# Modulation chunks folded in three places, and the bias diagonals shared between two engines, in a fused decoder trunk

## The reference, cut to what matters

```python
for l in range(DEPTH):
    mod = jax.nn.silu(c) @ ada_w[l] + ada_b[l]
    sh1, sc1, g1, sh2, sc2, g2 = jnp.split(mod[:, None, :], 6, axis=-1)
    h = rmsnorm(x, norm1_g[l]) * (1.0 + sc1) + sh1
    x = x + g1 * hybrid_mixer(h, positions, rel_bias, ...)
    h = rmsnorm(x, norm2_g[l]) * (1.0 + sc2) + sh2
    x = x + g2 * peer_ffn(h, ...)
```

## Time and profile before

| | |
|---|---|
| median of 3 runs | 2330.95 us (2330.95 to 2333.8) |
| profiled execution | 2331.92 us, span 2330.1 us |
| mean granted clock, share of full | 0.956 |
| busy | PE 2155.0 us, DVE 1545.6, ACT 1229.2, POOL 439.4 |
| DMA | 378.78 MB, mean 163 GB/s |

### The profile page before, as it was taken

How to read it: one execution, slowest core, us unless ns; L and a number is a source line. 1 busy time by engine, 2 the same in 40 slices (tenths; PEclk the granted TensorE clock), 3 DMA queues, 4 the chain that set the end, 5 groups by cost and what they waited for, 6 DMA issues and landing times.

```text
span 2330.1 us, 39430 instructions
## 1 busy us (share of the span) xinstructions
PE 2155.0 (92%) x13500; PEld 1948.3 (84%) x13500; DVE 1545.6 (66%) x3026; ACT 1229.2 (53%) x2330; POOL 439.4 (19%) x184
## 2 busy tenths in 40 slices
PE   5788779999999999999998877999999999999998
PEld 4677668999999988888877766899999998888886
DVE  7669436993577867777766943699347886555555
ACT  8622424555688854444442242445468885454553
POOL 0000016889300000000000001678930000000000
PEclk9789789999999999999999977999999999999999
DMA  7733034455444447777763303445544444556553
GB/s 257 264 100 100 28 129 136 154 181 172 144 136 144 142 142 259 263 266 256 266 223 106 100 28 109 132 154 182 170 140 145 139 137 131 195 191 194 193 191 107
DMA packets 103474, 378.78 MB, mean 163 GB/s; under 512 B 11488, under 2 KB 11872, under 8 KB 102880
## 3 DMA queue, kind: packets, MB, share of 16 engines
q1 hardware_dynamic: 102672, 373.74, 48.0%
q10 hardware_dynamic: 720, 4.00, 0.4%
HBM read 375.46 MB, written 2.23 MB: 162 GB/s over the span
## 4 chain that ended last, share of the span: by engine, by line
PE 65%; issue 14%; POOL 9%; DVE 7%; ACT 2%; DMA 2%; POOLq 0%; SPq 0%; DVEq 0%; ACTq 0%
PE bank L1626 30%; POOL split_lo L478 9%; PE bank L1529 7%; PE bank L1530 7%; PE bank L1531 7%; PE bank L1593 5%; PE bank L1318 3%; DMA ring<-stream 2%; PE bank L1281 1%; PE bank L1492 1%; PE bank L1292 1%; PE bank L1343 1%; DVE grid L841 1%; DVE grid L974 1%; PE bank L1616 1%
## 5 line engine op out<-in xcount | busy, mean ns | idle before, releaser
L1529 PE MATMUL bank<-h_hi,split_hi 128*128 128x256 f32 x2304 | 670.1, 291 | 40.6 <-DVE h_lo L1080 21.3
L1530 PE MATMUL bank<-h_lo,split_hi 128*128 128x256 f32 x2304 | 655.8, 285 | 0.0
L1531 PE MATMUL bank<-h_hi,split_lo 128*128 128x256 f32 x2304 | 655.8, 285 | 0.0
L1529 PEld LDWEIGHTS bank<-h_hi,split_hi 128*128 128x128 f32 x2304 | 445.5, 193 | 47.3 <-issue 24.4
L1184 DVE TENSOR_TENSOR split_lo<-ring,split_hi 128x1024 fp32r<-128x1024 f32 x248 | 303.9, 1225 | 257.8 <-ACT w_hi L759 257.8
L478 POOL TENSOR_TENSOR split_lo<-ring,split_hi 128x1024 fp32r<-128x1024 f32 x168 | 432.6, 2599 | 186.8 <-ACT split_hi L671 186.7
L758 ACT ACTIVATE split_hi<-ring 128x1024 fp32r<-128x1024 f32 x248 | 263.2, 1061 | 359.0 <-PE bank L1626 359.0
L1530 PEld LDWEIGHTS bank<-h_lo,split_hi 128*128 128x128 f32 x2304 | 446.3, 194 | 0.0
L1531 PEld LDWEIGHTS bank<-h_hi,split_lo 128*128 128x128 f32 x2304 | 445.5, 193 | 0.0
L671 ACT ACTIVATE split_hi<-ring 128x1024 fp32r<-128x1024 f32 x296 | 298.6, 1051 | 211.8 <-PE bank L1531 211.7
L1626 PE MATMUL bank<-split_hi,w_hi 128*128 128x512 f32 x1024 | 316.9, 391 | 0.0
(11 more groups left out here) (274 smaller groups left out, 2548.6 us busy)
## 6 DMA issues: line engine op xcount, KB each, us to landing
ring<-stream SPq DMA_DIRECT2D x658, 512.0 KB, 3.3
ada_ring<-stream SPq DMA_DIRECT2D x48, 512.0 KB, 4.1
spill<-tables ACTq DMA_DIRECT2D x1, 1152.0 KB, 5.3
tables<-spill ACTq DMA_DIRECT2D x1, 1152.0 KB, 7.3
xT<-x_in SPq DMA_DIRECT2D x1, 1024.0 KB, 9.7
s5raw<-s5w ACTq DMA_DIRECT2D x2, 512.0 KB, 5.6
y_out<-hT SPq DMA_DIRECT2D x1, 1024.0 KB, 3.9
KM<-mixc SPq DMA_DIRECT2D x1, 576.0 KB, 8.0
```

The costliest lines, as they stand in the source:

```text
L1529: mm(dst, hi, x_hi, start=start, stop=False, skip_group_check=not group)
L1530: mm(dst, hi, x_lo, start=False, stop=False, skip_group_check=not group)
L1531: return mm(dst, lo, x_hi, start=False, stop=stop, skip_group_check=not group)
```

## The change

Chunks 0 and 1 (shift and scale of the mixer's norm) are folded first, 16 blocks through the ring, with two masks behind each. Chunks 2, 3 and 4 go through a ring of their own (`mix_ring`, three slots) and are folded in one stretch on DVE, after the phases and ahead of the S5 coefficients; SP interleaves their fetches with those of the mixer's blocks (`mods_at`). PE sums them ahead of `turn(5)`. Chunk 5 is folded beside the second table of layer 0, ahead of the next layer's six; the turns there have 16 table blocks instead of 20, and are seven instead of six. Masks no longer share buffers: there is one for each threshold. Of the diagonals, ACT makes every third bucket's (11), POOL the others' (20), each in two multiplications of the identity by a broadcast column, 128 x 512 out. The norm of layer 0 is summed after bucket 8, the two modulation sums come after buckets 14 and 21, and the rope arguments move behind the norm's products. Before the first projection PE waits for `t5`. On SP's queue positions and constants come ahead of the ring, and x ahead of the small vectors.

```diff
-ADA_TURNS = (0, 2, 4, 6, 9, 11, 13, 15)
+ADA_TURNS = (0, 2, 4, 6, 8, 10, 12, 13)
+FIRST_ADA = 2 * KT
+MIX_ADA = 3 * KT
+SKIP = ADA - FIRST_ADA
+TURN = 16
+LATE_ADA = ADA // KT + 1
+MIX_SLOTS = 3
...
-diag = at_byte("diag", 48 * KB, [2, HEADS, 2, P], F32R)
+ge = at_byte("ge", 88 * KB + 4 * 16384, [BUCKETS - 1, P + T], F32R)
+diagA = at_byte("diagA", 56 * KB, [2, HEADS, 2, P], F32R)
+diagP = at_byte("diagP", 72 * KB, [2, HEADS, 2, P], F32R)
+mix_ring = at_byte("mix_ring", 36 * KB, [MIX_SLOTS, BLOCK])
+mix_acc = [at_byte(f"mix_acc{c}", at * KB, [BLOCK]) for c, at in enumerate((64, 72, 76))]
...
+def by_act(b):
+    return b % 3 == 0
...
     sp.dma_start(V[:, :], vec).then_inc(vec_in, 16)
+    sp.dma_start(posi, pos).then_inc(pos_in, 16)
+    sp.dma_start(K[:, :], consts).then_inc(const_in, 16)
     for s in range(RING):
         sp.dma_start(ring[:, s, :], stream[s]).then_inc(slot_filled[s], 16)
-        if s == 1:
-            sp.dma_start(K[:, :], consts).then_inc(const_in, 16)
-            sp.dma_start(posi, pos).then_inc(pos_in, 16)
-            sp.dma_start(S[:, :, :], small).then_inc(small_in, 16)
+    sp.dma_start(xT[:, :, :], x_in).then_inc(x_loaded, 16)
+    sp.dma_start(S[:, :, :], small).then_inc(small_in, 16)
     sp.dma_start(KM[:, :], mixc).then_inc(mixc_in, 16)
-    sp.dma_start(xT[:, :, :], x_in).then_inc(x_loaded, 16)
...
+    def fetch_first(n):
+        at = n if n < FIRST_ADA else n + SKIP
+        sp.dma_start(ring[:, n % RING, :], stream[at]).then_inc(slot_filled[n % RING], 16)
+    def fetch_mod(k):
+        if k >= MIX_SLOTS:
+            sp.wait_ge(ada_used, FIRST_ADA + k - MIX_SLOTS + 1)
+        sp.dma_start(mix_ring[:, k % MIX_SLOTS, :], stream[FIRST_ADA + k]).then_inc(mix_filled[k % MIX_SLOTS], 16)
...
-    segment(RING, ADA, ada_used, 0)
+    for j in range(FIRST_ADA):
+        sp.wait_ge(ada_used, j + 1)
+        fetch_first(RING + j)
+    for k in range(MIX_SLOTS):
+        fetch_mod(k)
+    mods_at = {2: (3, 4), 3: (5, 6, 7), 4: (8, 9, 10, 11), 5: (12, 13, 14, 15), 6: (16, 17, 18, 19), 7: (20, 21, 22, 23)}
+    for j in range(MIX):
+        sp.wait_ge(block_used, j + 1)
+        fetch_first(FIRST_ADA + RING + j)
+        for k in mods_at.get(j, ()):
+            fetch_mod(k)
...
-        with sp.Fori(0, ADA // KT, 1) as i:
-            for j in range(20):
-                sp.wait_ge(v_ready, i * 20 + (l * KEYS + SPLIT + j + 1))
+        def turn(i, at, source, used):
+            for j in range(TURN):
+                sp.wait_ge(v_ready, i * TURN + (l * KEYS + SPLIT + at + j + 1))
+                fetch(i * TURN + (late + RING + at + j), (late + RING + at + j) % RING)
                 if j in ADA_TURNS:
                     k = ADA_TURNS.index(j)
-                    sp.wait_ge(ada_used, i * 8 + (ADA + k - 1))
-                    sp.dma_start(ada_ring[:, k % 2, :], stream[bass.ds(i * 8 + (N_MAIN + l * ADA + k), 1)]
+                    sp.wait_ge(ada_used, i * KT + (used + k - 1))
+                    sp.dma_start(ada_ring[:, k % 2, :], stream[bass.ds(i * KT + (source + k), 1)]
                                  .rearrange("o p c -> (o p) c")).then_inc(ada_filled[k % 2], 16)
-        segment(late + RING + 120, LATE - 120, v_ready, l * KEYS + SPLIT + 120)
+        turn(0, 0, FIRST_ADA + MIX_ADA, FIRST_ADA + MIX_ADA)
+        with sp.Fori(0, ADA // KT, 1) as i:
+            turn(i, TURN, N_MAIN + l * ADA, ADA)
...
+    pool.wait_ge(const_in, 16)
+    pool.wait_ge(dist_ready, 1)
+    for n, b in enumerate(POOL_BUCKETS):
+        if n >= 2:
+            pool.wait_ge(bucket_added, POOL_BUCKETS[n - 2] + 1)
+        for part, d in enumerate((drel_hi[:, :].bitcast(F32), drel_lo)):
+            step = d[:, b * HEADS:b * HEADS + HEADS].rearrange("p (x y) -> p y x", x=2).unsqueeze(3).broadcast_to([P, 2, 2, P])
+            last = gp.tensor_tensor(diagP[:, n % 2, :, part, :].rearrange("p (y x) c -> p y x c", y=2),
+                                    ident.unsqueeze(1).unsqueeze(1).broadcast_to([P, 2, 2, P]), step, ALU.mult)
+        last.then_inc(pool_diag, 1)
...
+    for n in range(2):
+        diagonals(n)
+    act.wait_ge(x_loaded, 16)
+    squares(x_loaded, -1)
+    act.wait_ge(small_in, 16)
+    act.dma_start(s5raw[:, :], s5w[0]).then_inc(s5w_in, 16)
+    nc.scalar.activation(dt5, small_of(0, "ldt"), ACT.Exp).then_inc(s5_exp, 1)
+    for n in range(2, 5):
+        diagonals(n)
+    root(0, "ss1", D, rstd)
+    for n in range(5, len(ACT_BUCKETS)):
+        diagonals(n)
...
+        if l == 0:
+            act.wait_ge(rope_arg, 1)
+            nc.scalar.activation(rope[:, :, :], kw, ACT.Sin).then_inc(rope_sin, 1)
+            act.wait_ge(bucket_added, BUCKETS - 1)
+            for q in range(HEADS):
+                at = VEC_AT["rel"][0] + PERM[q]
+                nc.scalar.activation(t5[:, q, :], bank[:, 2 + q, 0:P + T], ACT.Identity, bias=V[:, at:at + 1]).then_inc(t5_ready, 1)
...
+    def fold(acc, b, k, used):
+        if k == 0:
+            ins = v.tensor_scalar(acc, b, siluc[:, 0:1], None, ALU.mult)
+        else:
+            dve.wait_ge(ada_used, used)
+            ins = v.scalar_tensor_tensor(acc, b, siluc[:, k:k + 1], acc, ALU.mult, ALU.add)
+        ins.then_inc(ada_used, 1)
+    for b in range(4):
+        reached(b)
     dve.wait_ge(silu_ready, 2)
+    for n in range(FIRST_ADA):
+        dve.wait_ge(slot_filled[n % RING], 16 * (n // RING + 1))
+        fold(g(ACC0 + n // KT * BLOCK, BLOCK), ring[:, n % RING, :], n % KT, n)
+        for b in range(4 + 2 * n, min(6 + 2 * n, BUCKETS - 1)):
+            reached(b)
+    def mix_step(n):
+        dve.wait_ge(mix_filled[n % MIX_SLOTS], 16 * (n // MIX_SLOTS + 1))
+        fold(mix_acc[n // KT][:, :], mix_ring[:, n % MIX_SLOTS, :], n % KT, FIRST_ADA + n)
...
+    dve.wait_ge(ada_columns, FIRST_ADA // KT)
+    add_biases(0, 0, FIRST_ADA, bank[:, 7, 0:FIRST_ADA])
...
             for k in range(KT):
                 v.tensor_tensor(sq[:, k, :], xT[:, k, :], rstd, ALU.mult).then_inc(xr_ready, 1)
-        if l:
-            dve.wait_ge(mixc_in, 16 * (l + 1))
+        if l == 0:
+            normed(l, "ss1")
+            rope_arguments()
+        dve.wait_ge(mixc_in, 16 * (l + 1))
...
+        if l == 0:
+            dve.wait_ge(bucket_added, BUCKETS - 1)
+            for n in range(MIX_ADA):
+                mix_step(n)
+            dve.wait_ge(rope_sin, 1)
+            for i in range(3):
+                last = v.tensor_scalar(rope[:, i, :], rope[:, i, :], const("mul")[:, i:i + 1], None, ALU.mult)
+            last.then_inc(rope_ready, 1)
+            dve.wait_ge(rope_ready, 1)
...
+        if l == 0:
+            dve.wait_ge(ada_columns, (FIRST_ADA + MIX_ADA) // KT)
+            add_biases(0, FIRST_ADA, MIX_ADA, bank[:, 6, T:T + MIX_ADA])
+        v.scalar_tensor_tensor(sc2, mod2[:, l, 4 * KT:5 * KT], 1.0, sm("n2g"), ALU.add, ALU.mult)
...
+        def turn(i, at, chunk):
+            for j in range(TURN):
+                low(i, TURN, at + j)
+                if j - 2 in ADA_TURNS:
+                    k = ADA_TURNS.index(j - 2)
+                    dve.wait_ge(ada_filled[k % 2], i * (16 * KT // 2) + 16 * (chunk * KT // 2 + k // 2 + 1))
+                    if k == 0:
+                        dve.wait_ge(ada_columns, i + ((FIRST_ADA + MIX_ADA) // KT + chunk))
+                    fold(ada_acc[:, :], ada_ring[:, k % 2, :], k, i * KT + (FIRST_ADA + MIX_ADA + chunk * KT + k))
         if l + 1 < DEPTH:
+            turn(0, 0, 0)
             with dve.Fori(0, ADA // KT, 1) as i:
+                turn(i, TURN, 1)
+            for j in range(LATE_ADA * TURN, LATE):
                 low(0, 0, j)
+            dve.wait_ge(ada_columns, (FIRST_ADA + MIX_ADA) // KT + LATE_ADA)
+            add_biases(l, 5 * KT, KT, bank[:, 0, 0:KT])
+            add_biases(l + 1, 0, ADA, bank[:, 0, KT:KT + ADA])
...
+    for b in range(BUCKETS - 1):
+        add_bucket(b)
+        if b == 8:
+            sums_of(0, "ss1", sq, KT, 0)
+        if b in (14, 21):
+            n = (14, 21).index(b)
+            pe.wait_ge(ada_used, (n + 1) * KT)
+            ada_sums(7, n, g(ACC0 + n * BLOCK, BLOCK))
...
+        else:
+            pe.wait_ge(t5_ready, HEADS)
...
+        if l == 0:
+            pe.wait_ge(pv_taken, 5)
+            pe.wait_ge(ada_used, FIRST_ADA + MIX_ADA)
+            for c in range(MIX_ADA // KT):
+                ada_sums(6, c, mix_acc[c], T)
         turn(5)
...
+            def turn(i, at, chunk):
+                output_rows(i, TURN, at)
+                pe.wait_ge(ada_used, i * KT + (FIRST_ADA + MIX_ADA + (chunk + 1) * KT))
+                ada_sums(0, i, ada_acc, chunk * KT)
+            turn(0, 0, 0)
             with pe.Fori(0, ADA // KT, 1) as i:
-                output_rows(i, 20, 0)
-                pe.wait_ge(ada_used, i * KT + ((l + 1) * ADA + KT))
-                ada_sums(0, i, ada_acc)
-            output_rows(0, 8, 120)
+                turn(i, TURN, 1)
+            output_rows(0, TURN, LATE_ADA * TURN)
```

(50 more changed lines are left out.)

133 lines of the change are left out of this document (45 added, 88 removed).

## The result

The changed kernel takes **2402.33 us** (median of four, 2401.41 to 2404.48) against 2330.95 of the kernel before: a ratio of 1.0306, 95% interval 1.0288 to 1.0323. The profiled execution took 2403.23 us, with a span of 2401.4, which is 71.3 more than the 2330.1 before. The sign was forecast, the size was not: +71 instead of +13, and outside the range.

A forecast was written before the change was run, and what follows sets the result against it. PE held 65% of the chain, and DVE's L899 at 156.26 us was the milestone moving the end. Terms 3.2 + 2.5 + 5.4 + 1.7 = +12.8 on the profiled 2331.92 gave 2344.5 us, range 2318 to 2370.

The forecast's parts named there:

- chunk 5 beside the second table: Table pass of layer 0: one more sum, +1.7 us, with the denser folds hidden by PE.
- rival 4: Table pass becomes DMA-bound: eight blocks of 0.52 MB add 16 us, 2360 us; chance 0.04.
- POOL's operation: Diagonals in the first stretch: each POOL multiplication takes 1.3 us, range 1.15 to 1.48.
- Rival 1: First stretch: DVE and POOL don't collide, or POOL's op is near 0.6 us; 2320.7 us, chance 0.18.
- rival 2: Diagonals: the broadcast operand costs POOL a full 2.40 us per operation, +40, 2384 us; chance 0.08.
- rival 5: Front: PE starts projecting early and the end doesn't move, 2331 us; chance 0.12.
- Second sum: First stretch: bucket 21 added near 58 us, PE then waits for the folds, second modulation sum done at 71.5.
- Norm, rope, phases: DVE after the second modulation sum: norm to 84.5 us, rope arguments and phases 27 more, to 111.5.
- Three folded chunks: 24 folds ahead of the state space, held by fetches: 47 us, to 158.5; milestone L899 at 159.5, +3.2.
- rival 3: The three folded chunks stream at DVE's speed, 30 us instead of 47: -17, 2327.5 us; chance 0.08.
- Cold restart: PE's second S5 block, after PE stands some 28 us: +2.5 us, bounds 0 to 3.7.
- Sums at the end of the attention: 48 matmul records ahead of turn(5): 7 us (5 to 8), less 1.63 of PE idle, +5.4.

The follow-up runs named there:

- experiment 1: The changed kernel with the last fold of each table-pass turn two rows earlier (six other folds move by one or two rows): 2340.56 us.
- experiment 6: The changed kernel with eleven slots instead of three for the 24 blocks folded ahead of the state space: 2384.05 us.
- experiments 1 and 3: The former has its own line; the latter is the changed kernel with the last fold of each turn one row earlier, not two: 2378.95 us.

## Why the prediction was wrong, step by step

*The step that failed* is "PE hides the folds (ten us of DVE, 4 MB); nothing else is late", of chunk 5 beside the second table: +1.7, measured +60. It counted what DVE and DMA have to do, and both had room, as experiment 1 confirms: with the last fold two rows earlier the pass costs 1.8. It didn't ask **in which place of the queues the last fold stands** and which of PE's rows it depends on. The diff said it: eight fetches spread over 16 rows instead of 20 end at index 13 of 16 instead of 15 of 20, and folds come two later, behind the last low part. My rival 4 put the table pass at risk for DMA's sake, 2360 us, and had the place right and the mechanism wrong.

The other terms, against the profile of the changed kernel:

- *Head of the queue*: diagonals start at 6.1 us; 6.0 was said.
- *POOL's operation*: 1.15 for 1.3, the low end of the forecast's own range; the eight norm products, which share the time with POOL's last operations, took 6.15 us for 11.2. Two-input folds beside it take 2.06 us and pairs of masks 2.30, so a round is 4.2 us (folds start at 17.20, 21.41, 25.62) and not 5.25. Rival 1, no collision, falls; rival 2 too. PE starts du0 at 85.9 (96 said), 42 us earlier than before, and the second S5 block still waits for DVE, so rival 5 comes nearest for the front.
- *Second sum*: bucket 21 near 53.3 (58 said), PE waits 6.53 us for the folds, sum done 63.4 (71.5 said).
- *Norm, rope, phases*: 38.5 us from the sum's end to 101.9, for 40; the end is 9.6 earlier than said, 8.1 of it from the sum.
- *Three folded chunks*: 49.7 us for 47. L965 comes at 152.4, 3.8 earlier instead of 3.2 later. It is held by fetches, as said, so rival 3 falls; experiment 6 prices the few slots at 18 us.
- *Cold restart*: the S5 block takes 5.66 for 3.69, so 2.0 for 2.5. The front as a whole gains 1.8 us where 5.7 were to be lost.
- *Sums at the end of the attention*: 10.24 us for 7, all 48 cold; less what the old wait took, 8.3, for +5.4. They had been priced at 2.3 us for 16, between the warm 1.68 and the front's 2.7 of the earlier trace rows, and took 3.4. From DVE's second S5 input to the last turn this trace has 13.1 us more than before, the traces of experiments 1 and 3 have 8.2 and 8.8: the sums are in all three, the other 4.8 went in cold stretches of this execution.

So front −1.8, end of the attention +13, table pass +60: 71.3 in the profiled execution. The forecast itself has a slip of 0.2: 2331.92 + 12.8 is 2344.7, not 2344.5.

Without the seam (experiment 1) the change costs 10.3 us, close to the 12.8 of the forecast. That is luck in part: the front was priced at +5.7 and gains 1.8 to 4.3 in the three traces, and the end of the attention was priced at +5.4 and costs 8.2 to 13.1. The direction came out as forecast, but most of the loss came from a place that had been put at 1.7.

The Trainium skill, page "SBUF — State Buffer", section "SBUF: two separate sides", speaks of an exclusive lock held for the full instruction. The first stretch nearly agrees: with 2.02 for POOL's 1.15 a fold of 1.28 costs it 0.87, so 0.41 of the fold fits beside it. The Trainium skill, page "GPSIMD Engine Reference", section "Elementwise — side-by-side cycle accounting", gives 4497 ns for two inputs of 2048 elements. The forecast's estimate for the operation, worked out from that and the 2.40 of the earlier trace rows, was 1.36; the trace has 1.15.

## What to carry to other kernels

When work of a second stream is woven into a pipeline with few slots, its last piece ahead of a join must stand so many rows before the join that the rows left cover the whole loop of slot freed, operands made, piece done; here 4.3 us, so two rows of 2.7. Spare time on every engine doesn't show that; the order in each queue does. And where a stand on PE is short, price the cold stretch behind it too: behind a mean wait of 2.2 us it was the larger part, 3.3 of 5.5 us.

## What the runs showed of the hardware

- PE stood for 1.53 us ahead of a sum, and the granted clock fell from 1.00 before the stand to 0.54 in the 4 us behind it, close to the lower of its two levels; a turn lost 5.5 us for 2.2 of mean wait. With the same sum and no stand it stayed at 1.00 (experiment 1).
- Behind a stand, one-column matmuls didn't bring the clock back: 48 of them took 10.37 us at 0.50, and the block behind them took 5.60 us where a warm one takes 3.69.
- Beside DVE's unbroken work POOL alternated with it, one operation each, in the changed kernel (folds 2.06 us, pairs of masks 2.30), and in the versions with 15 buckets on POOL one operation was kept out for 14.97 and 15.75 us. What decides between the two wasn't tried.
